# RWKV chunk solve: 64x64 chunk blocks held compactly and multiplied on diagonal quarters of the array

## What is computed

```python
def step(S, inp):
    r_t, w_t, k_t, v_t, kk_t, a_t = inp
    sa = jnp.einsum('bhij,bhj->bhi', S, -kk_t)
    S = (S * w_t[:, :, None, :] + sa[..., :, None] * (kk_t * a_t)[..., None, :]
         + v_t[..., :, None] * k_t[..., None, :])
    return S, jnp.einsum('bhij,bhj->bhi', S, r_t)
```

## Time and profile before

| | us |
|---|---|
| median of 3 runs | 5230.46 (5229.61 to 5240.97) |
| profiled execution | 5236.57 |
| its span, first to last instruction | 5234.9 |
| busy: TensorE, its weight loads | 4701.0, 3286.2 |
| busy: VectorE, ScalarE, GpSimdE | 2334.9, 1671.7, 711.4 |
| mean granted TensorE clock | 0.956 of full |
| mean rate of DMA | 56 GB/s |

### The profile page before, as it was taken

How to read it: one execution, slowest core, us unless ns; L and a number is a source line. 1 busy time by engine, 2 the same in 40 slices (tenths; PEclk the granted TensorE clock), 3 DMA queues, 4 the chain that set the end, 5 groups by cost and what they waited for, 6 DMA issues and landing times. The chain is left out here.

```text
span 5234.9 us, 67300 instructions
## 1 busy us (share of the span) xinstructions
PE 4701.0 (90%) x25200; PEld 3286.2 (63%) x25200; DVE 2334.9 (45%) x4864; ACT 1671.7 (32%) x3854; POOL 711.4 (14%) x938
## 2 busy tenths in 40 slices
PE   6898898797889998999969898987988899989999
PEld 2567566466666666777426575674566666667774
DVE  2355555434552453444224555553345534534342
ACT  2333232334552342212023332323345523421120
POOL 0000100000000004444000101000000000144430
PEclk9999999899999999999989999998999999999999
DMA  5001101201002103231240101012010011132322
GB/s 204 24 9 23 31 9 18 76 15 45 25 12 84 65 32 112 90 111 69 78 162 24 13 19 31 9 18 78 27 32 25 31 65 65 34 117 87 107 74 76
DMA packets 150418, 291.17 MB, mean 56 GB/s; under 512 B 53268, under 2 KB 79124, under 8 KB 144614
## 3 DMA queue, kind: packets, MB, share of 16 engines
q1 hardware_dynamic: 149976, 282.08, 16.6%
q10 hardware_dynamic: 112, 4.72, 0.2%
HBM read 239.41 MB, written 52.06 MB: 56 GB/s over the span
## 5 line engine op out<-in xcount | busy, mean ns | idle before, releaser
L974 PE MATMUL banks<-hT,w_piece 128*128 128x384 f32 x1536 | 558.1, 506 | 2.4 <-ACT raw L1078 2.3
L2143 PE MATMUL banks<-hT,w_piece 128*128 128x384 f32 x1152 | 390.0, 494 | 18.0 <-DMA w_piece<-in_w_cols 16.5
L974 PEld LDWEIGHTS banks<-hT,w_piece 128*128 128x128 f32 x1536 | 285.6, 197 | 175.8 <-issue 22.1
L2143 PEld LDWEIGHTS banks<-hT,w_piece 128*128 128x128 f32 x1152 | 216.6, 192 | 173.1 <-issue 20.9
L2432 PE MATMUL banks<-hT,w_gate 128*128 128x288 f32 x1152 | 300.6, 412 | 19.2 <-DMA w_gate<-in_w_cols 19.2
L2432 PEld LDWEIGHTS banks<-hT,w_gate 128*128 128x128 f32 x1152 | 222.4, 193 | 82.5 <-DMA w_gate<-in_w_cols 20.0
L2489 PE MATMUL banks<-hT,mergedT 128*128 128x512 f32 x576 | 247.5, 592 | 0.0
L1916 DVE SCALAR_TENSOR_TENSOR keysT<-banks,gains,rstd 64x128 f32<-64x128 f32 (+1 forms) x272 | 112.0, 412 | 259.0 <-ACT rstd L1830 256.5
L2535 DVE TENSOR_TENSOR gate_quarters<-gate_kept,banks 128x288 f32<-128x288 f32 x144 | 65.4, 454 | 325.9 <-PE banks L2432 322.9
L2498 ACT ACTIVATE gate_kept<-banks 128x288 f32<-128x288 f32 x144 | 59.1, 410 | 457.3 <-PE banks L2432 457.3
L2489 PEld LDWEIGHTS banks<-hT,mergedT 128*128 128x128 f32 x576 | 109.4, 190 | 137.0 <-issue 136.8
(11 more groups left out here) (370 smaller groups left out, 9808.7 us busy)
## 6 DMA issues: line engine op xcount, KB each, us to landing
w_gate<-in_w_cols SPq DMA_DIRECT2D x96, 512.0 KB, 4.0
w_piece<-in_w_cols SPq DMA_DIRECT2D x68, 512.0 KB, 4.3
w_ada<-in_w_ada SPq DMA_DIRECT2D x12, 2048.0 KB, 9.4
w_branch<-in_w_br SPq DMA_DIRECT2D x96, 256.0 KB, 2.8
y_branch<-y_gated SPq DMA_DIRECT2D x12, 1152.0 KB
sb_cached_keysT<-in_sbkT SPq DMA_DIRECT2D x8, 1024.0 KB, 6.9
sb_cached_values<-in_sbv SPq DMA_DIRECT2D x8, 1024.0 KB, 5.2
hT<-in_w_out SPq DMA_DIRECT2D x4, 2048.0 KB, 11.2
```

The lines of the kernel that those rows point to most:

```text
L974: last = mm(dst, w[0 if kind in ("k", "v") else 1][:, k, :], hT[:, k, c], start=(k == 0), stop=(k == KD - 1))
L2143: last = mm(ps[:, bank[n], 0:TG], w[wn % 3][:, k, :], hT[:, k, TG * g:TG * g + TG], start=(k == 0), stop=(k == KD - 1))
```

## The change

All matrices of the solve that were block-diagonal 128x128 are held as 64 columns: a tile keeps chunk 0 in partitions 0 to 63 and chunk 1 in 64 to 127. Each product is made block by block: chunk `r` reads partitions 64r to 64r+63 and writes the same partitions of PSUM, so that it uses 64 rows and 64 columns of the array, on the diagonal quarter r. Both chunks write the same bank, at different partitions. akv uses the two other quarters for the prompt, the scores all four (head by rows, chunk by columns, each head in a bank of its own). The lower product of the scores moves from bank 2 to spare columns of banks 0 and 1, and loses its semaphore. The masks become 64 columns wide, most copies and adds halve in width, `SC` shrinks to the k part (`KA`), and the power's transpose is masked straight from PSUM. The order of the work on each engine stays (`step` is now called `turn`). The sample tile's r scores go into a tile that is zeroed once a layer, in the stage before the first solve. The loaded constants shrink from 9520 to 6960 bytes a partition.

```diff
-                ("mask_p", 2 * P), ("mask_s", 2 * P), ("tri64", 64), ("masi_s", P),
-                ("dn_p", 2 * P), ("dn_s", 2 * P), ("dt16", P),
+                ("tri64", 64), ("tri16", 64), ("up64", 64), ("up16", 64), ("low16", 64), ("below16", 64), ("ident64", 64),
+                ("masi_s", P), ("dn_s", P),
...
+                own(nc.vector.memset(R.SS[:, :, :], 0.0))
...
-        SC = [sb(f"scores_a{s}", [P, 2, 2 * P]) for s in range(2)]
-        PW = [[sb(f"power1_{s}", [P, 2, 2 * P]) for s in range(2)], [sb("power2", [P, 2, 2 * P])] * 2, [sb("power4", [P, 2, 2 * P])] * 2]
-        P8 = sb("power8", [P, 2, P])
-        ET = [sb(f"inverseT{s}", [P, 2, P]) for s in range(2)]
-        LO = [sb(f"off_diagonal{s}", [P, 2, P]) for s in range(2)]
+        KA = [sb(f"scores_ka{s}", [P, 2, 64]) for s in range(2)]
+        PW = [[sb(f"power1_{s}", [P, 2, P]) for s in range(2)], [sb("power2", [P, 2, P])] * 2, [sb("power4", [P, 2, P])] * 2]
+        P8 = sb("power8", [P, 2, 64])
+        ET = [sb(f"inverseT{s}", [P, 2, 64]) for s in range(2)]
+        LO = [sb(f"off_diagonal{s}", [P, 2, 64]) for s in range(2)]
         RH = [sb(f"rhs{s}", [P, 2, P]) for s in range(2)]
-        XG = [sb(f"x_and_g{s}", [P, 2, 2, P]) for s in range(2)]
+        XG = [sb(f"x_and_g{s}", [P, 3 * P]) for s in range(2)]
...
+        def step(i, r, a, n):
+            return ps[HALVES[r], step_bank(i), a:a + n]
+
+        def inv(i, r, k, a, n):
+            return ps[HALVES[r], step_bank(i) + 1, 2 * P * (k % 2) + a:2 * P * (k % 2) + a + n]
...
-                score(0, 1).then_inc(scores_ready, 1)
+                for q in range(2):
+                    for r in range(2):
+                        tok = slice(P * i + 64 * r, P * i + 64 * r + 64)
+                        a = 1 - r if q == 1 and i < NPT else r
+                        for hh, hc in enumerate(HALVES):
+                            mm(ps[HALVES[r], hh, P * q:P * q + P].rearrange("p (s n) -> p s n", s=2), BK[hc, q, tok], RW[hc, i, a:a + 4:3, :], start=True, stop=True)
+                for r in range(2):
+                    tok = slice(P * i + 64 * r, P * i + 64 * r + 64)
+                    for hh, hc in enumerate(HALVES):
+                        last = mm(ps[HALVES[r], hh, 2 * P:2 * P + 64], RW[hc, i, r, :], BK[hc, 0, tok], start=True, stop=True)
+                last.then_inc(scores_ready, 1)
...
-                for hh in range(2):
-                    last = mm(ps[:, 3, 64 * hh:64 * hh + 64], SC[i % 2][:, hh, P:2 * P], TM[:, i, 2, 64 * hh:64 * hh + 64], start=True, stop=True)
+                for hh, hc in enumerate(HALVES):
+                    for c, cc in enumerate(HALVES):
+                        r = 1 - c if i < NPT else c
+                        last = mm(ps[HALVES[r], akv_bank(i, r), 64 * hh:64 * hh + 64], KA[i % 2][cc, hh, :], TM[cc, i, 2, hc], start=True, stop=True)
...
                 for hh in range(2):
-                    m, mt = PW[n][i % 2][:, hh, 0:P], PW[n][i % 2][:, hh, P:2 * P]
-                    if n < 2:
-                        mm(ps[:, step_bank(i), 2 * P * hh:2 * P * hh + P], mt, m, start=True, stop=True)
...
+                        m, mt = PW[n][i % 2][rc, hh, 0:64], PW[n][i % 2][rc, hh, 64:P]
+                        if n < 2:
+                            mm(step(i, r, P * hh, 64), mt, m, start=True, stop=True)
+                        else:
+                            last = mm(step(i, r, 64 * hh, 64), mt, m, start=True, stop=True)
+                    for r, rc in enumerate(HALVES):
+                        m, mt = PW[n][i % 2][rc, hh, 0:64], PW[n][i % 2][rc, hh, 64:P]
+                        if n < 2:
+                            last = mm(step(i, r, P * hh + 64, 64), m, mt, start=True, stop=True)
...
+                    for r, rc in enumerate(HALVES):
+                        p = P8[rc, hh, :] if k == 2 else PW[k + 1][i % 2][rc, hh, 0:64]
+                        last = mm(inv(i, r, k, 64 * hh, 64), p, ET[i % 2][rc, hh, :], start=True, stop=True)
...
-                    x = ps[:, step_bank(i), :].rearrange("p (k h n) -> p k h n", k=2, h=2)
...
-                            mm(x[:, 0, hh, :], LO[i % 2][:, hh, :], ET[i % 2][:, hh, :], start=True, stop=True)
...
+                            for r, rc in enumerate(HALVES):
+                                mm(step(i, r, 64 * hh, 64), LO[i % 2][rc, hh, :], ET[i % 2][rc, hh, :], start=True, stop=True)
+                        for r, rc in enumerate(HALVES):
+                            last = mm(step(i, r, P + P * hh, P), ET[i % 2][rc, hh, :], RH[i % 2][rc, hh, :], start=True, stop=True)
...
-                        rhs = XG[i % 2][:, 1, hh, :] if k == 5 else Q[:, hh, :]
-                        last = mm(half(i, k)[:, hh, :], XG[i % 2][:, 0, hh, :], rhs, start=True, stop=True)
+                        for r, rc in enumerate(HALVES):
+                            rhs = G[i % 2][rc, hh, :] if k == 5 else Q[rc, hh, :]
+                            last = mm(out(i, r, k, P * hh, P), X[i % 2][rc, hh, :], rhs, start=True, stop=True)
                     last.then_inc(q_ready, 1)
...
+                dst, w = (PW[n + 1][0], 2 * P) if n < 2 else (P8, P)
+                for rc, bank in read_parts(i):
+                    last = copy(dst[rc, :, :].rearrange("p h n -> p (h n)"), ps[rc, bank, 0:w], ACT.Copy)
+                last.then_inc(power_copied, 1)
...
+                a = 0 if i < NPT else P
+                for rc, bank in read_parts(i):
+                    last = copy(XG[i % 2][rc, a:3 * P], ps[rc, bank, a:3 * P], ACT.Copy)
...
+                    own(V.tensor_tensor(KA[s][:, :, :], ps[:, 0:2, P:P + 64], bc("up16" if i == NPT else "up64"), ALU.mult), sc_masked)
...
+                        if i == NPT:
+                            dst = SS[rc, :, :].rearrange("p h (q n) -> p h q n", q=2)[:, :, :, 64 * r:64 * r + 64]
+                        else:
+                            dst = SI[rc, i, :, :].rearrange("p h (q n) -> p h q n", q=2)
+                            if r == 0:
+                                dst = dst[:, :, ::-1, :]
+                        tri = con("tri16" if i == NPT else "tri64")[rc].unsqueeze(1).unsqueeze(1).broadcast_to([64, 2, 2, 64])
+                        last = V.tensor_tensor(dst, src, tri, ALU.mult)
+                    last.then_inc(scores_read, 1)
                 elif k == 2:
...
+                    V.tensor_tensor(PW[0][s][:, :, 0:64], low, bc("low16"), ALU.mult)
...
+                    V.tensor_tensor(LO[s][:, :, :], low, bc("below16"), ALU.mult)
                 else:
...
+                    if i >= 2:
+                        dve.wait_ge(xg_ready, i - 1)
+                    own(V.tensor_tensor(PW[0][s][:, :, 64:P], ps[:, 0:2, 0:64], bc("up16"), ALU.mult))
+                    own(V.tensor_tensor(ET[s][:, :, :], PW[0][s][:, :, 64:P], bc("ident64"), ALU.add), masked)
```

More of the change, by code:

```diff
@@ L67, in shape_constants @@
     c["sbpass"] = f(col >= row)
[L68 to L80, removed]
+    near = row // TS == col // TS
+    c["masi_s"], c["dn_s"] = f(near & (row <= col)), f(near & (row > col))
+    in_chunk, at = row % 64, np.arange(64)[None]
+    same16 = in_chunk // 16 == at // 16
+    c["tri64"], c["tri16"] = f(in_chunk <= at), f(same16 & (in_chunk <= at))
+    c["up64"], c["up16"] = f(in_chunk < at), f(same16 & (in_chunk < at))
+    c["low16"], c["below16"] = f(same16 & (in_chunk > at)), f(~same16 & (in_chunk > at))
+    c["ident64"] = f(in_chunk == at)
     t = np.arange(T)
@@ L507, in token_shift @@
         own(nc.vector.scalar_tensor_tensor(oo[i], dd[i], mu, cur[i], ALU.mult, ALU.add))
+HALVES = (slice(0, 64), slice(64, P))
 def rwkv_solve(nc, S, A, l, ps, con, T_, h, nx):
@@ L536, in step_bank, with akv_bank, read_parts, akv_parts @@
             return 4 + 2 * (i % 2)
-        def half(i, k):
-            return ps[:, step_bank(i) + 1, 2 * P * (k % 2):2 * P * (k % 2) + 2 * P].rearrange("p (h n) -> p h n", h=2)
+        def akv_bank(i, r):
+            return 3
+        def step(i, r, a, n):
+            return ps[HALVES[r], step_bank(i), a:a + n]
+        def inv(i, r, k, a, n):
+            return ps[HALVES[r], step_bank(i) + 1, 2 * P * (k % 2) + a:2 * P * (k % 2) + a + n]
+        out = inv
+        def read_parts(i):
+            return ((slice(0, P), step_bank(i)),)
+        def akv_parts(i):
+            return ((slice(0, P), 3),)
+        def inv_parts(i, k):
+            return ((slice(0, P), ps[:, step_bank(i) + 1, 2 * P * (k % 2):2 * P * (k % 2) + P]),)
+        def out_parts(i, k):
+            return ((slice(0, P), ps[:, step_bank(i) + 1, 2 * P * (k % 2):2 * P * (k % 2) + 2 * P]),)
+        def by_head(ap):
+            return ap.rearrange("p (h n) -> p h n", h=2)
         @block.tensor
@@ L545, in scores @@
                     return
[L546 to L556, removed]
                 if i >= 1:
@@ L608, in inverse, with turn @@
                 for hh in range(2):
-                    p = P8[:, hh, :] if k == 2 else PW[k + 1][i % 2][:, hh, 0:P]
```

(27 more changed lines are left out.)

80 lines of the change are left out of this document (25 added, 55 removed).

## The result

The changed kernel takes 5007.67 us (median of four runs, 4993.7 to 5022.59), against 5230.92 for the kernel before (5229.61 to 5240.97): ratio 0.956, 95% interval 0.954 to 0.959. The profiled execution took 5002.3 around a span of 5000.6.

What follows compares the result with a forecast made beforehand. The solve stages were taken as bound by the number of TensorE passes times their pace; tiles of 7.0 us instead of 9.38 and stage ends save 21 us a stage, 168 in eight, giving 5062 us, range 5035 to 5085.

Steps and rivals of the forecast that it cites:

- The pace of quarter pairs: Solve products on TensorE: two diagonal quarters run together, 0.057 us per pair for 64 moving columns, 0.11 for 128.
- The rival of the shared bank: Solve products: quarters writing one bank follow each other, 10.05 us a tile, 5255 us in all; chance 0.11.
- issue rival: TensorE in the solve: issuing passes bounds, so the change does nothing, about 5230 us; chance 0.04.
- ScalarE's stretch: Copies of x and g, rows and first power hold back the second power until 2.33 us after g's last pass starts.
- The ends of a stage: Where one tile runs alone: 2.0 us saved a stage, and some 0.5 for narrower first masks and scores.
- The eight starts of a tile: Per solve stage, 2.4 us saved at each tile start, less 0.8 for the first: 18.4 us.
- what I took off for the first tile: 0.8 us less saving per stage, as the first tile has no tile before it to solve.
- The slow starts of the clock: Four solve stages begin at the lower clock level and take 3.5 us more; forecast to stay.
- Akv: In a tile's solve: 4 pairs, 0.23 us of TensorE time, counted in the sum.
- The waits named: TensorE waits for ScalarE's first power copy before the second power, and for x and g before q's first product.
- partial overlap: Rival: pairs overlap in part, at 0.075 and 0.115 us, 0.6 more a tile, 5100 us in all; chance 0.12.
- scores in pairs: Scores run two quarters at a time, 1.1 us instead of 0.55; a tile is then 7.1 us instead of 7.0.

Runs made afterwards that it cites:

- e1: Changed kernel with the inverse's products of the two chunks in two banks, VectorE's add split in two instructions: 5052.1 us, tile 7.27 against 6.70.
- e7: Changed kernel with one row tile copied a second time on ScalarE, ahead of the first power copy: 5019.9 us, tile 6.87 against 6.70.
- e5: Changed kernel with ScalarE's three row copies moved behind its first power copy: 4979.5 us, tile 6.46 against 6.70.
- e6: Changed kernel with the next tile's scores moved ahead of q's first product on TensorE: 5017.1 us, tile 6.70 as before the move.
- e8: Changed kernel run again as is: 5021.3 us; its line, over all runs: time outside solve stages is 4346 us plus 0.41 of the time at lower clock.
- e2: Changed kernel with all passes of one quarter issued before the other's in power, inverse, akv, x and g, and q: 5067.4 us, tile 7.39 against 6.70.
- e3: Changed kernel with akv's eight passes issued twice: 5024.8 us, tile 6.70 unchanged.

## Why the prediction was right in kind and short in size

The profiled span fell by 234.3 us, where 168 were forecast. The 66 us between them:

*The pace of quarter pairs: right.* 0.057 for 64 moving columns was forecast, and 0.026 to 0.029 a pass measured (lines 633 and 620); 0.11 for 128 (line 674 at 249.48, 249.59, 249.70); scores four at a time, 24 passes from 247.78 to 248.5. 147 passes a tile and 1285 a stage came as counted. The rival of the shared bank falls by this and by e1. The Trainium skill ("TensorEngine Tiling (Array Packing)", Gotcha 1: PSUM Pressure) says that row tiles cannot access the same bank at once; here two quarters in different rows that write different partitions of one bank run at full pace, so the measurement decides against that rule for this case. Of the issue rival, a pass each 0.046 us over a whole tile (6.70 / 147) shows that it had nothing.

*ScalarE's stretch: the term mis-sized.* Between the last pass of g and the second power I had 2.33 us; it is 2.09 (246.52 + 0.39 - 0.27 = 246.64, to 248.73). I added durations, 0.49 + 1.04 + 0.38 and gaps, 1.94 in all; from the start of the first copy (246.96) to the end of the last (248.68) are 1.72. The start of a copy follows the last one's by 0.38 for one that lasts 0.49, and by 0.28 for 0.27, so only the two long ones overlap what follows. Before shows it already, in order of time, in rows that I had not set against their durations:

```profile
252.38 0.49 ACT L684 ACTIVATE bk_and_vu_rows<-banks 128x384 f32<-128x384 f32 x1
...
252.77 0.59 ACT L692 ACTIVATE power<-banks 128x512 f32<-128x512 f32 x1
```

There 0.39 lie between the starts, though the first lasts 0.49. e7 shows that the tile hangs on this stretch one for one (0.17 for 0.17), e5 that releasing the second power from it shortens the tile, and e6 that time saved ahead of it does not. The rest of the tile was 0.06 too long in the sum (last pass of g at 6.97, called 7.0, and 4.61 from the second power on instead of 4.64). 0.30 a tile by eight tiles and eight stages is 19 us.

*The ends of a stage: undercounted.* The eight starts of a tile gave 21.4 us (six of 9.38 to 6.70, then 9.38 to 6.22 and 7.89 to 5.72) instead of 18.4. Of the 3.0 more, 2.4 is the term above and 0.8 is what I took off for the first tile, which was not there, less 0.2 of rounding (9.38 less 7.0 is 2.38, not 2.4). From a stage's start to its first g it was 3.95 us (11.66 to 7.71) instead of 2.5. I had allowed 0.5 for the narrower first masks and scores. From the start of the stage to the first power it is 2.24 us instead of 3.80: the first scores stand alone there, and so does the row of masks, 1.56 together. With both, a stage that starts at full clock gave 25.4 instead of 21: 36 us in eight, of which 19 are the term above and 17 the ends.

*The slow starts of the clock: wrong.* I let them stay. The seven other stages stood 16.5 us together above the shortest before (eight times 87.52 from 716.67), and stand 9.6 above it after (eight times 62.08 from 506.27): 7 us. The lower level granted inside the stages is 45 us before and 36 after: four stages before began with 9.5 us of it and two with 3.3, six after with 5.0 to 6.5. And each us of it cost less, 0.27 instead of 0.37.

*Akv, and scores beside q: not foreseen, and worth nothing here.* I laid akv (0.23) behind q. It ran beside it, and TensorE then waited for VectorE's add (250.20 + 0.42) before q's third product at 250.68, 1.95 us behind the second power; I had 1.93.

*Outside the stages: not foreseen.* 23.9 us, 19 of them the clock's by e8's line and the rest within its scatter; e8, with the clock as before, shows no effect of the change there.

19 + 17 + 7 + 24 make the 66 but for rounding. The waits named, VectorE's 4.31 us a tile (4.4 forecast), ScalarE's 2.80 (3.0) and ScalarE's copies of 382, 273 and 490 ns (383, 277 and 490) came as the prediction had them.

So the mechanism was right, and the step that failed is the sizing of the sum's terms: ScalarE's stretch first (2.33 us, measured 2.09), then a stage's ends and the slow starts. The range failed with the sum: it was built from terms that could only come out dearer (partial overlap, scores in pairs), and reached 32 us below the forecast, less than 36 of stage terms and 7 of clock.

## What to carry to other kernels

Where a chain of copies holds an engine up, take the distances between their starts, not the sum of their durations: both stand in the same rows. When passes go to several quarters of the array, write them in turns, because TensorE started passes only about four ahead of the program's order (e2). Count what a stage's start and end cost row by row, since nothing lies beside them there, and set apart what stretches untouched by a change gain or lose, together with their granted clock, before calling it the change's.

## What the runs showed of the hardware

- Two 64x64 quarters in different rows write one PSUM bank, at different partitions, at the pace of two banks: eight passes of 64 columns in 0.40 us either way (e1).
- Diagonal and off-diagonal quarters run at once: six passes, two of 128 and four of 64 moving columns, in each 0.11 us (e3).
- A pass may start ahead of about four others of the program that wait for a busy quarter (e2).
- ScalarE's copies from PSUM can overlap: 0.38 us between starts for one of 384 columns that lasts 0.49, and 0.16 behind one of 128 columns that lasts 0.27, where both have 128 partitions (e7, and the last tile of each stage); before a copy of 64 partitions it was 0.28.
- One kernel's stretches of the same work differ by 8 us in 115 with the granted clock (0.98 against 0.90), and its executions by over 30 in 5000.
